# A mixer's sequence transform by one 512-column matrix, its mirrored half copied backwards, with the memory's transposes ahead of it

## What is computed

```
z = h @ w_in                                   # 1024 -> b_gate, c_gate, v, u, 512 columns each
y_conv = b_gate * short_conv3(c_gate * v, conv_w)
uf = u.reshape(1, 512, 8, 64)
y_fft = jnp.fft.fftn(uf, axes=(1, 3), norm="ortho").real
y = concat([rmsnorm(y_conv, g_conv_out), rmsnorm(y_fft, g_fft_out)])
x = x + y @ w_out
...
k = rmsnorm(mem, norm_mem) @ w_k               # memory: 256 rows of 1024
v = rmsnorm(mem, norm_mem) @ w_v
...
top_v, top_i = top_k(logits, 4)                # 32 experts, each token goes to 4
```

## Time and profile before

| | us |
|---|---|
| median of three runs | 2207.1 (2205.42 to 2207.76) |
| the profiled execution, its own time | 2204.74 |
| its span in the trace | 2202.8 |
| TensorE busy | 2075.9 (94%) |
| VectorE, ScalarE, GpSimd busy | 865.7, 478.9, 359.7 |
| mean granted TensorE clock | 0.97 |

### The profile page before, as it was taken

The page is one execution under the profiler, slowest core; times in us unless marked ns, Lnnn a source line. Parts: engine busy times, 40 slices in busy tenths (PEclk is TensorE's granted clock), DMA queues, the critical chain, the costliest instruction groups (busy, mean ns, idle before and its releaser), DMA issues.

```text
span 2202.8 us, 41891 instructions
## 1 busy us (share of the span) xinstructions
PE 2075.9 (94%) x17404; PEld 1255.0 (57%) x17404; DVE 865.7 (39%) x1468; ACT 478.9 (22%) x749; POOL 359.7 (16%) x389
## 2 busy tenths in 40 slices
PE   6999898499999999999999999979998998999998
PEld 5879777234344434433443333337775777888887
DVE  4444434432333233333333333333565433444444
ACT  4242333000000000000000000023445723122221
POOL 1010001112222222222223222231201200000000
PEclk9999999699999999999999999979998999999999
DMA  6325111999999999999999999973111022233230
GB/s 235 116 77 166 58 39 40 354 348 403 405 404 410 405 405 405 410 403 404 403 405 402 404 408 396 399 256 106 58 58 39 1 65 70 76 99 111 77 113 38
DMA packets 157840, 521.53 MB, mean 237 GB/s; under 512 B 16428, under 2 KB 71776, under 8 KB 124928
## 3 DMA queue, kind: packets, MB, share of 16 engines
q1 hardware_dynamic: 137008, 496.01, 57.7%
q0 software_dynamic: 20784, 24.85, 4.7%
HBM read 510.65 MB, written 18.88 MB: 240 GB/s over the span
## 4 chain that ended last, share of the span: by engine, by line
PE 60%; DMA 9%; SPq 4%; DVE 3%; ACT 2%; POOL 1%; issue 1%; ACTq 0%; DVEq 0%; POOLq 0%
PE ps L1970 21%; PE ps L1984 11%; PE ps L390 8%; PE ps L392 8%; PE ps L391 8%; DMA ring_a<-in_w_down 6%; SPq L567 3%; DMA ring_a<-in_w_gate_up 2%; SPq L565 2%; PE ps L1879 1%; PE ps L492 1%; POOL rstd L464 1%; PE ps L1871 1%; PE ps L1889 1%; PE ps L1832 0%
## 5 line engine op out<-in xcount | busy, mean ns | idle before, releaser
L1970 PE MATMUL ps<-ring_a,xe 128*32 128x512 f32 x3912 | 436.0, 596 | 12.2 <-DVE xe L1579 10.6
L1984 PE MATMUL ps<-ring_a,act_t 128*32 128x256 f32 x6000 | 333.5, 379 | 5.5 <-DMA ring_a<-in_w_down 3.8
L1970 PEld LDWEIGHTS ps<-ring_a,xe 128*32 128x32 f32 x3912 | 124.8, 110 | 297.0 <-issue 254.3
L1984 PEld LDWEIGHTS ps<-ring_a,act_t 128*32 128x32 f32 x6000 | 193.6, 110 | 153.0 <-issue 21.5
L1970 PE MATMUL ps<-ring_b,xe 128*32 128x512 f32 x2232 | 251.5, 593 | 0.0
L390 PE MATMUL ps<-xt_hi,hi 128*128 128x512 f32 x576 | 228.8, 397 | 5.6 <-DVE xt_lo L505 4.7
L392 PE MATMUL ps<-xt_hi,lo 128*128 128x512 f32 x576 | 226.4, 393 | 0.0
L391 PE MATMUL ps<-xt_lo,hi 128*128 128x512 f32 x576 | 226.2, 393 | 0.0
L1073 ACT ACTIVATE glu<-glu 128x768 f32<-128x768 f32 x32 | 27.0, 843 | 649.1 <-DVE glu L1586 649.1
L757 POOL DMA_INDIRECT x_rows<-ye,idx x96 | 154.3, 1607 | 37.8 <-issue 37.8
L390 PE MATMUL ps<-hi,xt_hi 128*128 128x512 f32 (+1 forms) x384 | 147.4, 384 | 7.4 <-DVE lo L377 5.2
(11 more groups left out here) (297 smaller groups left out, 2475.4 us busy)
## 6 DMA issues: line engine op xcount, KB each, us to landing
ring_a<-in_w_gate_up SPq DMA_DIRECT2D x163, 1024.0 KB, 20.8
ring_a<-in_w_down SPq DMA_DIRECT2D x125, 1024.0 KB, 23.5
ring_b<-in_w_gate_up SPq DMA_DIRECT2D x93, 1024.0 KB, 19.5
raw<-in_w_in SPq DMA_DIRECT2D x20, 1024.0 KB, 7.7
raw<-in_w_gate SPq DMA_DIRECT2D x11, 1024.0 KB, 5.4
raw<-in_w_up SPq DMA_DIRECT2D x11, 1024.0 KB, 5.4
raw<-in_w_down SPq DMA_DIRECT2D x11, 1024.0 KB, 4.8
raw<-in_w_out SPq DMA_DIRECT2D x8, 1024.0 KB, 5.0
```

The costliest lines, as they stand in the source:

```text
L1970: last = pe.matmul(ps[QUAD * j:QUAD * j + QUAD, g, :], xe[:, g, QUAD * k:QUAD * k + QUAD], w[:, j, :, :, :], start=k == 0, stop=k == KT - 1)
L1984: last = pe.matmul(y_block(g, j), act_t[:, g, QUAD * (2 * c + h):QUAD * (2 * c + h) + QUAD], w[:, h, QF * j:QF * j + QF], start=c == 0 and ...
```

## The change

The two matrices become one of 512 columns: columns 0 to 256 of Cs, then columns 1 to 255 of Ss. The stream has 29 chunks, so each later chunk moves up by one (`A_K` from 10 to 9). TensorE runs four transform groups instead of eight. Of each, ScalarE copies columns 0 to 256 to `pc` and columns 255 down to 1 behind them (step of minus one, semaphore `dft_cos`); then VectorE copies the 255 sine columns to `psn[1:256]` and, times minus one and backwards, to `psn[257:512]`, and releases the bank. Columns 0 and 256 of `psn` are set to zero once.

The memory's transposes stand ahead of the transform on TensorE, and their splits (L501, L505 of before) ahead of the mixer's last halves on ScalarE and VectorE. The squares and halves of the convolution stand ahead of the copies instead of behind them. The channel matmuls write to the bank that the tile's own transform used (0 to 3), and so the first four key groups each wait for one `mixer_lo`.

```diff
--- before.py
+++ after.py
@@ -36,6 +36,7 @@
 EPS_1, EPS_2 = 1e-5, 1e-6
 LAMBDA_INIT = 0.8 - 0.6 * math.exp(0.0)
 ALPHA, LIMIT = 1.702, 7.0
+HALF = SEQ // 2
 SILU_TOP = ALPHA * LIMIT / (1.0 + math.exp(-ALPHA * LIMIT))
 MASKED = -1e30
 
@@ -77,7 +78,8 @@
     c[:, C_EYE:] = n[None, :] % NE == p[:, None] % NE
     s = np.arange(SEQ)
     w = 2 * np.pi * (np.outer(s, s) % SEQ) / SEQ
-    dft = np.stack([np.cos(w), np.sin(w)]).astype(np.float32) * np.float32(SEQ ** -0.5)
+    half = SEQ // 2
+    dft = np.concatenate([np.cos(w)[:, :half + 1], np.sin(w)[:, 1:half]], axis=1).astype(np.float32) * np.float32(SEQ ** -0.5)
     rel = np.arange(SPAN) - (SEQ - 1)
     dist = np.abs(rel)
     far = np.maximum(dist, 1).astype(np.float32)
@@ -269,13 +271,13 @@
         w_in, w_out = A["w_in"][0], A["w_out"][0]
         src_a = [half_rows(w_in, i, 1536) for i in range(2)]
         src_a += [cols(w_in, 256 * i) for i in (2, 3, 4, 5, 0, 1)]
-        src_a += [A["dft"][i].rearrange("(k p) n -> p k n", p=P) for i in range(2)]
+        src_a += [A["dft"].rearrange("(k p) n -> p k n", p=P)]
         src_a += [cols(A[w][0], 256 * i) for w in ("w_k", "w_v") for i in range(4)]
         src_a += [half_rows(w_out, i) for i in range(4)]
         src_a += [cols(A["w_q"][0], 256 * i) for i in range(4)]
         src_a += [half_rows(A["w_o"][0], i) for i in range(4)]
-        A_U, A_C, A_V, A_B, A_DFT, A_K, A_VM, A_OUT, A_Q, A_O, A_END = 0, 2, 4, 6, 8, 10, 14, 18, 22, 26, 30
-        SA = Stream(nc, ctx, "a", src_a, [4] * 2 + [2] * 6 + [4] * 2 + [2] * 8 + [4] * 4 + [2] * 4 + [4] * 4,
+        A_U, A_C, A_V, A_B, A_DFT, A_K, A_VM, A_OUT, A_Q, A_O, A_END = 0, 2, 4, 6, 8, 9, 13, 17, 21, 25, 29
+        SA = Stream(nc, ctx, "a", src_a, [4] * 2 + [2] * 6 + [4] + [2] * 8 + [4] * 4 + [2] * 4 + [4] * 4,
                     row_halves=(A_U, A_O, A_O + 2))
 
         SA.two_banks, SA.two_from = range(SA.first[A_Q], SA.first[A_O]), 0
...
@@ -789,6 +791,13 @@
                     for t in range(MT):
                         act.wait_ge(mem_in[t], 16)
                         norm_squares(act, NS["mem"] + t, v_mem[:, t, :])
+                if c == A_DFT:
+
+                    for f in range(T):
+                        evacuated(act, SA, SA.first[A_B] + f)
+                        act.activation(cv[:, f, 1:SEQ + 1], y_conv[:, f, :], ACT.Square)
+                        act.activation(xt_hi[:, f, :], y_conv[:, f, :], ACT.Copy,
+                                       scale=scal[:, S_GC + f:S_GC + f + 1]).then_inc(mixer_hi, 1)
                 for g in range(SA.first[c], SA.first[c + 1]):
                     n = g - SA.first[c]
                     if c in SA.row_halves:
@@ -802,27 +811,20 @@
                         copy(cv[:, 2 * (c - A_C) + n, 1:SEQ + 1], ps[:, g % 4, :]).then_inc(SA.evacuated[g % 4], 1)
                     elif c == A_DFT:
                         act.wait_ge(SA.group_done, g + 1)
-                        copy(pc[:, n, :], ps[:, g % 4, :]).then_inc(SA.evacuated[g % 4], 1)
+                        copy(pc[:, n, 0:HALF + 1], ps[:, g % 4, 0:HALF + 1])
+                        copy(pc[:, n, HALF + 1:SEQ], ps[:, g % 4, HALF - 1:0:-1]).then_inc(dft_cos, 1)
                     elif A_K <= c < A_VM:
                         act.wait_ge(SA.group_done, g + 1)
                         act.wait_ge(mixer_lo, T)
                         copy(kT[:, 2 * (c - A_K) + n, :], ps[:, g % 4, 0:MEM]).then_inc(SA.evacuated[g % 4], 1)
                 if c == A_DFT:
-
-
-                    for f in range(T):
-                        evacuated(act, SA, SA.first[A_B] + f)
-                        act.activation(cv[:, f, 1:SEQ + 1], y_conv[:, f, :], ACT.Square)
-                        act.activation(xt_hi[:, f, :], y_conv[:, f, :], ACT.Copy,
-                                       scale=scal[:, S_GC + f:S_GC + f + 1]).then_inc(mixer_hi, 1)
-                if c == A_DFT + 1:
+                    for t in range(MT):
+                        norm_hi(act, NS["mem"] + t, tile(mt_hi, t))
                     for f in range(T):
                         act.wait_ge(fft_done, f + 1)
-                        act.activation(pc[:, f, :], ps[:, 4 + f % 2, :], ACT.Square)
-                        act.activation(xt_hi[:, T + f, :], ps[:, 4 + f % 2, :], ACT.Copy,
+                        act.activation(pc[:, f, :], ps[:, f, :], ACT.Square)
+                        act.activation(xt_hi[:, T + f, :], ps[:, f, :], ACT.Copy,
                                        scale=scal[:, S_GF + f:S_GF + f + 1]).then_inc(mixer_hi, 1)
-                    for t in range(MT):
-                        norm_hi(act, NS["mem"] + t, tile(mt_hi, t))
             def norm_behind_chunk(name, S, c):
 
                 def squares(t):
@@ -1157,6 +1159,12 @@
                     dve.wait_ge(gain_in[1], 16)
                     for t in range(MT):
                         norm_rows(dve, NS["mem"] + t, v_mem[:, t, :], 1)
+                if c == A_DFT:
+                    dve.memset(psn[:, :, 0:HALF + 1:HALF], 0.0)
+                    for f in range(T):
+                        dve.wait_ge(mixer_hi, f + 1)
+                        dve.scalar_tensor_tensor(xt_lo[:, f, :], y_conv[:, f, :], scal[:, S_GC + f:S_GC + f + 1],
+                                                 xt_hi[:, f, :].bitcast(F32), ALU.mult, ALU.subtract).then_inc(mixer_lo, 1)
                 for g in range(SA.first[c], SA.first[c + 1]):
                     n = g - SA.first[c]
                     if c in SA.row_halves:
@@ -1181,9 +1189,11 @@
                             link(dve.scalar_tensor_tensor(y, cv[:, f, k:k + SEQ], w(k), y, ALU.mult, ALU.add))
                         dve.wait_ge(SA.group_done, g + 1)
                         dve.tensor_tensor(y, ps[:, g % 4, :], y, ALU.mult).then_inc(SA.evacuated[g % 4], 1)
-                    elif c == A_DFT + 1:
-                        dve.wait_ge(SA.group_done, g + 1)
-                        dve.tensor_copy(psn[:, n, :], ps[:, g % 4, :]).then_inc(SA.evacuated[g % 4], 1)
+                    elif c == A_DFT:
+                        dve.wait_ge(dft_cos, n + 1)
+                        dve.tensor_copy(psn[:, n, 1:HALF], ps[:, g % 4, HALF + 1:SEQ])
+                        dve.tensor_scalar(psn[:, n, HALF + 1:SEQ], ps[:, g % 4, SEQ - 1:HALF:-1], -1.0, None, ALU.mult)\
+                           .then_inc(SA.evacuated[g % 4], 1)
                     elif A_VM <= c < A_OUT:
                         dve.wait_ge(SA.group_done, g + 1)
                         if c == A_VM:
@@ -1191,17 +1201,12 @@
                         dve.tensor_copy(v_mem[:, n, 256 * (c - A_VM):256 * (c - A_VM) + 256], ps[:, g % 4, 0:256])\
                            .then_inc(SA.evacuated[g % 4], 1)
                 if c == A_DFT:
-                    for f in range(T):
-                        dve.wait_ge(mixer_hi, f + 1)
-                        dve.scalar_tensor_tensor(xt_lo[:, f, :], y_conv[:, f, :], scal[:, S_GC + f:S_GC + f + 1],
-                                                 xt_hi[:, f, :].bitcast(F32), ALU.mult, ALU.subtract).then_inc(mixer_lo, 1)
-                if c == A_DFT + 1:
+                    for t in range(MT):
+                        norm_lo(dve, NS["mem"] + t, tile(mt_hi, t), tile(mt_lo, t))
                     for f in range(T):
                         dve.wait_ge(mixer_hi, T + f + 1)
-                        dve.scalar_tensor_tensor(xt_lo[:, T + f, :], ps[:, 4 + f % 2, :], scal[:, S_GF + f:S_GF + f + 1],
+                        dve.scalar_tensor_tensor(xt_lo[:, T + f, :], ps[:, f, :], scal[:, S_GF + f:S_GF + f + 1],
                                                  xt_hi[:, T + f, :].bitcast(F32), ALU.mult, ALU.subtract).then_inc(mixer_lo, 1)
-                    for t in range(MT):
-                        norm_lo(dve, NS["mem"] + t, tile(mt_hi, t), tile(mt_lo, t))
             dve.wait_ge(ssq_done, 1)
             dve.tensor_copy(ss[:, 40:48], ps[:, 6, 0:8]).then_inc(ssq_sb, 1)
             dve.wait_ge(mix_rstd, 1)
@@ -1667,10 +1672,13 @@
                     else:
                         group_features(pe, SA, c, g, xt_hi, xt_lo, SEQ)
 
+            for t in range(MT):
+                pe.wait_ge(n_h, NS["mem"] + t + 1)
+                norm_transpose(pe, NS["mem"] + t, hbuf[:, t % 2, :])
             evacuated(pe, SA, 7)
             for g in range(4, 7):
                 evacuated(pe, SA, g)
-            for c in (A_DFT, A_DFT + 1):
+            for c in (A_DFT,):
                 pe.wait_ge(SA.lo_ready, c + 1)
                 wh, wl = part(hi, c % HL, T), part(lo, c % HL, T)
                 for g in range(SA.first[c], SA.first[c + 1]):
@@ -1683,19 +1691,14 @@
 
             for f in range(T):
                 evacuated(pe, SA, SA.first[A_DFT] + f)
-                evacuated(pe, SA, SA.first[A_DFT + 1] + f)
-                if f >= 2:
-                    pe.wait_ge(mixer_lo, T + f - 1)
-                mm(ps[:, 4 + f % 2, :], cc(C_BDC), pc[:, f, :], start=True, stop=False)
```

(9 more changed lines are left out.)

2 lines of the change are left out of this document (1 added, 1 removed).

## The result

| | before | after |
|---|---|---|
| median of 4 runs of each, us | 2206.26 | 2184.91 (2183.57 to 2185.22) |
| profiled execution, own time | 2204.74 | 2184.85 |
| its span | 2202.8 | 2182.8 |
| TensorE busy | 2075.9 | 2061.7 |

The ratio is 0.9903 [0.9888, 0.9919]: 21.4 us faster, with an interval of 17.9 to 24.7 us.

The account below looks back on a forecast made before the run. TensorE, busy 94% of the span, was taken as the bound. Keys 16.9 us earlier plus 1.5 of low clock give 18.4: 2204.7 becomes 2186.3, plus 2.4 for the median, 2188.7 us; range 2185.2 to 2191.8.

Parts of the forecast that it names:

- The seam: TensorE's idle stretch before the key projection: keys start at 132.5 instead of 149.4, and 1.5 us of low clock goes.
- The transposes: The memory's 16 transposes, moved ahead of the mixer's transform on TensorE, taken at 1.7 us.
- The transform: One mixer transform instead of two: 48 matmuls go, saving 10.9 us; the remaining one also takes 10.9 us.
- The channel matmuls: Four tiles after the transform, each in its own bank without waits for `mixer_lo`, counted at 7.1 us.
- the rival of the low clock: Half clock stays at the key projection, so only 16.9 us are saved: 2190.2 us; chance 0.10.
- the late chain: Reversed reads over 1.7 us dearer than forward make the fourth tile wait; at 3 us, about 2195; chance 0.04.
- the slower case: Reversed reads 6 us dearer make ScalarE the bound and start the keys past 155, over 4.4 us slower; chance 0.02.
- `lo` of the next chunk: VectorE's split of chunk 11, ending at 138.2, perhaps 139.3 beside GpSimd's sums; wanted at 144, so hidden.
- Forecast for the place: Mixer transform to key projection: 16.9 us from the earlier key start plus 1.5 us of low clock, together 18.4.
- the surcharge of 2.4: Whole kernel: the old median's 2.4 us above the profiled execution, added to 2186.3 to forecast the new median.
- I therefore pass an earlier key projection on to the end at full size: Behind the seam nothing holds the time fixed, so the 18.4 us gain reaches the kernel's end in full.
- The experts' second pass: Expert stage: changed rounding could give an expert over 96 tokens, needing one more pass, 31.5 us; part of 0.02.

Follow-up runs that it names:

- seam_filled: Kernel before the change, plus nine matmuls of unread constants in the two idle stretches of the seam; 2204.17 us, ratio 0.9991.
- before_again: Kernel before the change, repeated without edit for another profile; 2207.03 us in one run, span 2205.0.
- moves_only: Kernel before, still two matrices, with memory transposes ahead of the transform, a bank per tile and waits at the key groups; 2197.11 us, ratio 0.9962.
- mirror_only: Changed kernel with one matrix and mirrored copies, but channel matmuls and memory transposes put back as before; 2191.65 us, ratio 0.9934.
- again: Changed kernel, repeated without edit; 2184.10 us, ratio 0.9901.
- after_late8: Changed kernel with eight matmuls of 256 constant columns ahead of the memory's transposes, a 3.4 us delay; 2187.80 us, ratio 0.9916.

## Why the prediction was right, and where it was wrong

**The seam: right, part by part.** The transposes took 1.66 us (112.47 to 114.13) for 1.7. The transform took 10.98 for 10.9. The keys ran steadily from 132.09, 132.4 on the old clock, for 132.5. The channel matmuls took 6.86 for 7.1: the tail of the last ran beneath the first key matmul. The clock stayed at 1.00, so the rival of the low clock, 0.10, did not come, and seam_filled shows why: the idle time made it. A reversed read costs what a forward one does; the late chain would have needed 1.7 us more a read and found none, and the slower case, with its 6 us, is as far away. `lo` of the next chunk took 3.07 us beside GpSimd's sums and ended at 138.6 on the old clock, between the 138.2 and the 139.3 that the prediction gave it. Forecast for the place 18.4, measured 18.7.

**The step that failed is the last of the sum: "The median of the runs, 2207.1, lies 2.4 above that execution; the forecast for the median is 2188.7."** From the profiled execution I had 2204.74 - 18.4 = 2186.3, and the changed kernel's profiled one took 2184.85: 1.5 too high. The other 2.3 are the surcharge of 2.4, of which the changed kernel showed 0.06. It was no constant that one kernel hands to the next. Part was the sample: over 58 timed runs of before beside the experiments the median is 2205.6, 1.5 below that of my three. The other 0.9 lies between executions, and before_again shows one way: a stall may be followed by a short low clock or a long one, and the one profiled had a short one. But the seam's stall is not what makes before scatter. seam_filled and moves_only have a clock of 1.00 at the seam and still spread over 6.2 and 4.8 us, and mirror_only, which keeps the stall, over 2.2. With one matrix the runs of a kernel spread over 1.1 to 3.0 us (4 or 5 runs), with 30 chunks over 3.7 to 10.1 (5 to 15 runs beside the experiments); why is open. I carried the surcharge over unchanged. The range was not worked out either: its named terms reach 2.0 us below the forecast (1.7 of scatter, 0.1 of the transposes, 0.2 of the tails), and it was set 3.5 below.

**The 1.5** are 0.3 that the execution was ahead of the seam, 0.3 of the seam itself, and 0.9 that "I therefore pass an earlier key projection on to the end at full size" left out. That was nearly true, but by two errors of opposite sign: the gain shrinks from 19.0 at the value copy to 18.3 at the last `ff_a`, and grows by the 1.6 of the last wait. Against the other pair, before_again and again, it is 20.0, 20.9 and 22.5 at these places, so a good part of this is the execution; the 1.6 is not. A price of 1.5 us for a stall's low clock stood in my own sum for one stall, and I did not ask what the kernel's other stalls pay and whether it could change. A range that reached 2 us lower for this would have held the time.

**The forecast gain by itself**, 18.4 us, lies within the measured 17.9 to 24.7, near its lower end. It was short by 1.5 us against the two profiled executions and by 3.0 against the medians. The experts' second pass did not come.

## What to carry to other kernels

A gain at one place adds up well from rows: matmuls by their step, waits by their brackets, and the low clock behind a stall by the matmuls that it let through. Where the evacuating engines stand in the queue decides whether fewer matmuls are worth anything: 48 matmuls fewer gave 11.1 us with the copies in time, and 4.1 with the copies behind a split. And a single execution of a kernel with stalls is a draw, and so is the median of three: their distance is no constant to be added to the forecast of another kernel, and the range must hold both.

## What the hardware showed that I had not expected

- A wait of 2.45 us on TensorE was followed by half clock in seven of fourteen traces, which cost 1.6 us on top (the end); two waits of 2.10 and 2.63 us at the seam cost 1.5 us. Matmuls that nobody reads in the wait kept the clock at 1.00, and around the norms they made the changed kernel some 9 us faster.
- Whether the low clock comes, and for how long, can differ from execution to execution (0.91 and 0.72 at the seam), and can also be fixed for a kernel (0.90 or 1.00 in the last 16.5 us, seven traces each), with equal rows for the 322 us up to the wait. The two families differ ahead of that, by a VectorE instruction that starts 0.35 us later and by 0.6 us between the last half clock and the wait.
- Reads from PSUM with a step of minus one cost nothing extra on ScalarE or VectorE: 0.41 us for 255 columns on VectorE, forward 0.42.
- A quarter of the columns took half the time: a record of the constants' matmuls takes 0.11 us with 64 columns (96 in 10.8 us) and 0.23 with 256 (16 in 3.61 us, in after_late8).
